# A decoder layer with product-key experts on one core: the gates stage's one-hots built for 8 tokens at a time in bf16

## The reference, cut to what matters

```
v1, i1 = lax.top_k(s1, PEER_TOPK);  v2, i2 = lax.top_k(s2, PEER_TOPK)
sc, ci = lax.top_k(cand, PEER_TOPK)          # cand: all sums v1 + v2
e1 = take(i1, ci // PEER_TOPK);  e2 = take(i2, ci % PEER_TOPK)
eid = e1 * N_KEYS + e2                       # N_KEYS = 128
gate = jax.nn.softmax(sc, axis=-1)
act = gelu(einsum('chkd,cd->chk', exp_u[eid], xc))
out = einsum('chk,chkd->cd', gate * act, exp_v[eid])
```

## Time and profile before

| | us |
|---|---|
| median of 3 executions | 2285.61 (2278.62 to 2299.04) |
| the profiled execution | 2285.57 |
| its span, first to last instruction | 2283.8 |
| TensorE / VectorE / ScalarE / GpSimd busy | 2038.0 / 1499.3 / 612.3 / 390.5 |
| the gates stage, first `hot` to `h_low` | 846.65 to 1034.73 |

### The profile page before, as it was taken

The page is one execution under the profiler, slowest core; times in us unless marked ns, Lnnn a source line. Parts: engine busy times, 40 slices in busy tenths (PEclk is TensorE's granted clock), DMA queues, the critical chain, the costliest instruction groups (busy, mean ns, idle before and its releaser), DMA issues. The chain is left out here.

```text
span 2283.8 us, 29284 instructions
## 1 busy us (share of the span) xinstructions
PE 2038.0 (89%) x9849; PEld 1774.4 (78%) x9849; DVE 1499.3 (66%) x3828; ACT 612.3 (27%) x1012; POOL 390.5 (17%) x473
## 2 busy tenths in 40 slices
PE   7997899999995029996699999999999999999994
PEld 6884566774773016665699999999999999999993
DVE  1122943102799989994777768767777777777773
ACT  2121323101111013332233333333333333333332
POOL 0000000000122220000322222222232222332320
PEclk9999556769997559998899999999999999999997
DMA  7002301220120003334877768878688786877853
GB/s 307 17 16 76 129 1 42 97 88 0 57 94 0 0 1 148 148 148 166 271 245 267 248 231 260 270 234 269 212 290 265 242 269 212 295 253 251 268 188 114
DMA packets 195603, 381.98 MB, mean 167 GB/s; under 512 B 12992, under 2 KB 134782, under 8 KB 192094
## 3 DMA queue, kind: packets, MB, share of 16 engines
q1 hardware_dynamic: 157557, 243.52, 30.8%
q0 software_dynamic: 36864, 134.23, 17.6%
q10 hardware_dynamic: 1056, 2.62, 0.3%
HBM read 345.21 MB, written 35.34 MB: 167 GB/s over the span
## 5 line engine op out<-in xcount | busy, mean ns | idle before, releaser
L1374 PE MATMUL a_ps<-h_high,u_high 128*128 128x416 f32 x1024 | 359.1, 351 | 42.2 <-DVE u_low L1513 40.0
L1392 PE MATMUL y_ps<-p_high,v_high 128*128 128x416 f32 x1024 | 359.7, 351 | 4.4 <-DVE v_low L1513 2.2
L1374 PE MATMUL a_ps<-h_low,u_high 128*128 128x416 f32 x1024 | 361.4, 353 | 0.0
L1392 PE MATMUL y_ps<-p_high,v_low 128*128 128x416 f32 x1024 | 360.5, 352 | 0.0
L1374 PE MATMUL a_ps<-h_high,u_low 128*128 128x416 f32 x1024 | 358.5, 350 | 0.0
L1392 PE MATMUL y_ps<-p_low,v_high 128*128 128x416 f32 x1024 | 358.2, 350 | 0.0
L1479 POOL DMA_INDIRECT rows<-in_u_rows,row_u x128 | 140.8, 1100 | 663.2 <-DVE dots L1566 326.3
L1479 POOL DMA_INDIRECT rows<-in_v,row_u x128 | 173.5, 1355 | 406.9 <-DVE y L1562 322.4
L1374 PEld LDWEIGHTS a_ps<-h_high,u_high 128*128 128x128 f32 x1024 | 192.9, 188 | 48.2 <-DVE u_low L1513 26.1
L392 PE MATMUL proj<-w_in_sb,xT 128*128 128x256 f32 (+1 forms) x880 | 193.5, 382 | 14.6 <-DVE xT L290 12.8
L1535 DVE TENSOR_TENSOR gel<-gel,gate 128x416 f32<-128x416 f32 x128 | 75.7, 591 | 197.2 <-ACT gel L1432 196.9
(11 more groups left out here) (194 smaller groups left out, 2769.7 us busy)
## 6 DMA issues: line engine op xcount, KB each, us to landing
u<-in_uT SPq DMA_DIRECT2D x128, 512.0 KB, 4.3
vv<-in_v SPq DMA_DIRECT2D x128, 512.0 KB, 4.7
gates_kept<-staged SPq DMA_DIRECT2D x13, 2048.0 KB, 6.2
gate<-gates_kept SPq DMA_DIRECT2D x32, 832.0 KB, 7.1
w_in_sb<-in_w_in SPq DMA_DIRECT2D x4, 2048.0 KB, 21.6
wq<-in_w_q SPq DMA_DIRECT2D x16, 512.0 KB, 3.3
ckT<-in_ckT SPq DMA_DIRECT2D x8, 768.0 KB, 5.7
cv<-in_cv SPq DMA_DIRECT2D x8, 768.0 KB, 5.3
```

Of the source, the lines that this page charges most:

```text
L1374: ins = pe.matmul(a_ps[c % 2][:, 0:DT], x[:, c % 2, k], y, start=(k == 0 and n == 0), stop=(k == KT - 1 and n == 2))
L1392: ins = pe.matmul(y_ps[m % 4][:, 0:DT], x[:, of % 2, c, at:at + P], y, start=(c == 0 and n == 0), stop=(c == CG - 1 and n == 2))
```

## The change

The 416 tokens are taken in 52 batches of TB = 8. Per batch DVE issues five tensor_tensor over 128x1024 in bf16 with the token as the innermost axis: `hot` (comparison of `count`, the numbers 0 to 127 each repeated 8 times, with `e1b`, the 8 tokens' values repeated for each number), `here` (the same with `e2b`), and three products of `here` with the three parts of the weight, `placed[..., 0 to 2]`. The weight is split ahead of the loop into three bf16 parts whose sum is the f32 value exactly (`w3`). PE then issues, per token, three bf16 products with the same `hot`, accumulated in the same quarter bank; a column of a token's tables lies 8 elements (16 bytes) behind the one before. The ring of `hot` is 4 batches, `placed` has 2. `staged` is moved over `gate`, `p_high` and part of `p_low`, which are not used in this stage, to make room.

```
-            for t in range(DT):
-                at = P + t
-                wait(dve, g_done, t - HOTS + 1)
-                nc.vector.tensor_scalar(hot[:, t % HOTS], iota_f[:], e1T[:, at:at + 1], None, ALU.is_equal)
-                nc.vector.tensor_scalar(placed[:, t % HOTS], iota_f[:], e2T[:, at:at + 1], wT[:, at:at + 1],
-                                        ALU.is_equal, ALU.mult).then_inc(hot_ready, 1)
+            nc.vector.tensor_copy(e1b[:], e1T[:])
+            nc.vector.tensor_copy(e2b[:], e2T[:])
+            nc.vector.tensor_copy(count[:], spread(iota_f[:].rearrange("p (k o) -> p k o", o=1), [P, NK, TB])
+                                  ).then_inc(w_split, 1)
+            nc.vector.tensor_copy(w3[:, 0], wT[:]).then_inc(w_split, 1)
+            dve.wait_ge(w_split, 2)
+            nc.vector.tensor_tensor(rest[:], wT[:], w3[:, 0], ALU.subtract).then_inc(w_split, 1)
+            dve.wait_ge(w_split, 3)
+            nc.vector.tensor_copy(w3[:, 1], rest[:]).then_inc(w_split, 1)
+            dve.wait_ge(w_split, 4)
+            nc.vector.tensor_tensor(w3[:, 2], rest[:], w3[:, 1], ALU.subtract).then_inc(w_split, 1)
+            dve.wait_ge(w_split, 5)
+
+            def batch(x, n):
+                return spread(x[:, P + n * TB:P + (n + 1) * TB].rearrange("p (o t) -> p o t", o=1), [P, NK, TB])
+
+            for n in range(BATCHES):
+                wait(dve, g_done, TB * (n - HOTS + 1))
+                nc.vector.tensor_tensor(hot[:, n % HOTS], count[:], batch(e1b, n), ALU.is_equal)
+                wait(dve, hot_ready, 2 * n)
+                nc.vector.tensor_tensor(here[:], count[:], batch(e2b, n), ALU.is_equal).then_inc(hot_ready, 1)
+                wait(dve, g_done, TB * (n - 1))
+                dve.wait_ge(hot_ready, 2 * n + 1)
+                for i in range(3):
+                    ins = nc.vector.tensor_tensor(placed[:, n % 2, i], here[:], batch(w3[:, i], n), ALU.mult)
+                ins.then_inc(hot_ready, 1)
...
-                pe.matmul(g_ps[bank % GBANKS][:, t % GT * NK:(t % GT + 1) * NK], hot[:, t % HOTS], placed[:, t % HOTS],
-                          start=True, stop=True).then_inc(g_done, 1)
+                for i in range(3):
+                    ins = pe.matmul(g_ps[bank % GBANKS][:, t % GT * NK:(t % GT + 1) * NK], hot[:, n % HOTS, :, at],
+                                    placed[:, n % 2, i, :, at], start=(i == 0), stop=(i == 2))
+                ins.then_inc(g_done, 1)
```

More of the change, by code:

```diff
@@ L61 @@
 GT = 4
+TB = 8
+BATCHES = DT // TB
 GB = 32
 NB = DT // GB
-HOTS = 6
+HOTS = 4
 GBANKS = 4
@@ L1244, in experts @@
         gates_kept = nc.dram_tensor("gates_kept", (NB, P, NK, GB), F32, kind="Internal").ap()
+        staged = nc.alloc_sbuf_tensor_at("staged", [P, 2, NK, GB], F32, offset=-(-nc.sbuf_base // 32) * 32)
         gate = sb("gate", [P, 2, NB, CG, GB])
-        staged = sb("staged", [P, 2, NK, GB])
         p_high = sb("p_high", [P, 2 * CG, DT], F32R)
@@ L1259, in experts @@
         coef_p = sb("coef_p", [P, FPP])
-        hot = sb("hot", [P, HOTS, NK])
-        placed = sb("placed", [P, HOTS, NK])
+        hot = sb("hot", [P, HOTS, NK, TB], BF16)
+        here = sb("here", [P, NK, TB], BF16)
+        placed = sb("placed", [P, 2, 3, NK, TB], BF16)
+        count = sb("count", [P, NK, TB], BF16)
+        e1b = sb("e1b", [P, T], BF16)
+        e2b = sb("e2b", [P, T], BF16)
+        w3 = sb("w3", [P, 3, T], BF16)
+        rest = sb("rest", [P, T])
         iota_f = sb("iota_f", [P, NK])
@@ L1273, in experts @@
         hot_ready, g_done, g_taken = sem("hot_ready"), sem("g_done"), sem("g_taken")
+        w_split = sem("w_split")
         gates_stored = [sem(f"gates_stored{b}") for b in range(2)]
@@ L1396, in _ @@
             for t in range(DT):
-                bank = t // GT
-                pe.wait_ge(hot_ready, t + 1)
+                bank, (n, at) = t // GT, divmod(t, TB)
+                pe.wait_ge(hot_ready, 2 * (n + 1))
                 if t % GT == 0:
                     wait(pe, g_taken, bank - GBANKS + 1)
-                pe.matmul(g_ps[bank % GBANKS][:, t % GT * NK:(t % GT + 1) * NK], hot[:, t % HOTS], placed[:, t % HOTS],
-                          start=True, stop=True).then_inc(g_done, 1)
+                for i in range(3):
+                    ins = pe.matmul(g_ps[bank % GBANKS][:, t % GT * NK:(t % GT + 1) * NK], hot[:, n % HOTS, :, at],
+                                    placed[:, n % 2, i, :, at], start=(i == 0), stop=(i == 2))
+                ins.then_inc(g_done, 1)
             pe.wait_ge(g_taken, DT // GT)
```

## The result

| | before | after |
|---|---|---|
| median us | 2288.49 (2278.62 to 2299.04, 4 runs) | 2401.45 (2379.46 to 2408.39, 4 runs) |
| the profiled execution's span | 2283.8 | 2377.4 |
| gates stage, from DVE's first instruction behind the two clears to the start of the last copy of `staged` | 846.65 to 1035.38 = 188.7 | 829.03 to 1128.74 = 299.7 |

The account below looks back on a forecast made before the run. DVE was taken to set the gates stage's pace: 2285.57 - 22.8 (DVE) + 2.3 (last burst) = 2265.1 us, plus one for small waits, forecast 2266. Range 2254 to 2292 (own case 2256 to 2272, chance 0.72).

Parts of the forecast that it names:

- DVE's new instructions: Gates stage, five per batch of 8 tokens: 0.68 us each, about 0.60 from start to start.
- The seven instructions ahead of the loop: DVE's copies, casts and subtractions before the gates loop, on the path: 3.6 us (bounds 3.6 and 4.2).
- The wait of `placed` for `here`: First `placed` of each batch waits for the instruction right ahead: 0.03 us, overlap lost, the pair costs 0.71.
- Rival 1: Gates loop on DVE: the wait for `here` costs 0.27 instead of 0.03, 12.5 us lost, 2278 us; chance 0.13.
- PE's price per pair: Weight load and matmul of 128 bf16 columns in the gates stage: 0.109 us, so a burst of 24 takes 2.6.
- The point from which PE binds: Gates loop: PE begins to bind at 0.130 us per pair; at 0.146 the whole gain is eaten.
- The second rival: Gates loop, PE becomes the bound: spread columns or 1.2 GHz, no overlap, pair up to 0.214, 2371 us; chance 0.10.
- The clock: PE's granted clock in the gates stage of the changed profile: expected at 1.00.
- The last burst: End of the gates stage, PE's uncovered final burst before the last copy: 2.9 us, or 2.3 us more than before.
- What follows the stage: Handover and expert stage after the last copy: unchanged, so what the last copy gains, the kernel's end gains.
- The gain that the change was built on: DVE's part of the gates stage ends 22.8 us sooner, at 0.389 us per token in the loop against 0.452.
- rivals 2 and 3: Rival 3: DVE runs its new instructions at one element per step, 5.8 us per batch, 2405 us; chance 0.05.

Follow-up runs that it names:

- the kernels with a fast reader: The changed kernel with PE's moving operand read from neighbouring columns: both operands neighbouring 2276.09 us, only the moving operand 2275.31 us.
- the kernel with GpSimd: The changed kernel laid out in runs of 4 tokens (columns 8 bytes apart), third product's table made on GpSimd instead of DVE: 2335.08 us, ratio 1.0184.
- the experiment with one product of three: The changed kernel with only the first of a token's three products read 16 bytes apart, the other two from neighbouring columns: 2278.91 us (1 run).

## Why the prediction was wrong, point by point

- **DVE's new instructions**: right. 0.685 us each (0.68 forecast), 0.60 from start to start, by the row of `hit` with the same type and form. The seven instructions ahead of the loop took 832.74-829.03 = 3.7 us (3.6 forecast).
- **The wait of `placed` for `here`**: too small. 0.79 from start to start, not 0.71. In the changed kernel's first batch, where `placed` waits for `here` alone, the gap behind `here` was 0.04 (833.35+0.68 to 834.07). With neighbouring columns, from the third batch on, where it waits for `g_done` too, the gap was 0.11 (932.41+0.68 to 933.20), though those products had long been done. My sum had one wait at 0.03; the batch came to 3.20 in place of 3.11: 52*0.09 = 4.7 us. That the second wait makes the difference is read from where the gap changes, and it holds only with `here` right ahead: with `hot` between, the same two waits left no gap. Rival 1, with 0.27, would have been more; the truth lay between. This is the reason why the kernels with a fast reader came out at 172 and not at 168.2, the 188.7-22.8+2.3 of my sum.
- **PE's price per pair**: this is the step that failed. I took 0.109 from the nearest row in shape, the turns of line 380, and bounded it by 0.058 and 0.218. The row's columns lie side by side, and its 128 f32 columns are read at 4 bytes; the new operand's lie 16 bytes apart. I had written that no row tests this, and then let a row that differs in just this point give the value. For neighbouring columns my value was twice too high (0.056 measured, my bound from below), for the spread ones less than half: 0.234, above even my upper bound. What failed is the step by which a burst is 2.6 us, lies under DVE's 3.11 and hides behind the next batch: it took 5.62 us and set the pace of all 52 batches. The point from which PE binds, 0.130 per pair, fits: at 0.118 the time is DVE's, at 0.234 it is PE's.
- **The second rival** was the right mechanism in its first part and came out near in size: 2371 forecast, 2401 measured, by a loop of 52*5.62 = 292 us where I had 267. That it came so near is in part luck: it doubled a pair of 0.107, which was itself twice too high, while the spread operand made four times the 0.056; and the missing overlap of load and matmul that it also asked for is ruled out. The spread operand alone makes the 0.234, at 0.50, and 0.23 to 0.24 at 1.00. Since I thought that several things had to come together, I gave it one chance in ten.
- **The clock**: I expected 1.00 in the stage. From 900 to 1000 us it was 0.50 wherever all products were spread, and 1.00 with neighbouring columns or columns 4 or 8 bytes apart in batches of 8, but for the kernel with GpSimd (0.59); with batches of 16 it was 0.90. The 0.50 of the changed kernel cost nothing by itself there, as the experiment with one product of three and the first bursts show.
- **The last burst**: 2.3 us more was forecast, for 0.109 per pair. With PE behind, it became 9.4 us from `h_low` to the last copy, four banks of backlog.
- **What follows the stage**: right, nothing changed (1248 and 1249 us).
- The gain that the change was built on is there, 17 us of stage as soon as the columns lie 4 bytes apart, 15 at 8 bytes.
- Two slips in the numbers change nothing: rivals 2 and 3 together have 0.15, not 0.14, and the "0.107 of a full-clock pair" in rival 2 is the 0.109 of line 380.

## What to carry to other kernels

Ask of every matmul how far apart, in bytes, the columns of its moving operand lie. A layout that makes a neighbour engine's instruction long and dense (token innermost) can make PE's operand sparse, and PE then pays: up to 16 bytes in proportion to the distance from 4 bytes on, to about four times the price of neighbours for bf16 in these runs; runs of two to four tokens gave DVE the same dense instructions and PE its full or half rate. And when a price is read off a nearest row, write down in which property the row differs: if it is the one that the change introduces, the row bounds nothing.

## What the runs showed of the hardware that I had not expected

- The price of 128 moving bf16 columns by their distance: 0.056 us (2 bytes), 0.058 (4), 0.118 (8), 0.234 (16), 0.23 to 0.24 (32). Spread weights cost next to nothing: 0.062 against 0.056 per pair.
- From 8 bytes on that price is the same at both levels of the clock: 0.234 at 0.50 and 0.23 to 0.24 at 1.00 for 16 bytes, 2.99 us at 0.50 and 3.02 at 1.00 for 24 products at 8 bytes. For neighbouring columns it is not: 0.106 at 0.50, 0.056 at 1.00. PE never idled in the records from 836 to 1128 us, and its clock sat at 1.2 GHz all the time.
- Of two bf16 tensor_tensor of DVE that ran beside one of GpSimd (2.40 us), the first took its usual 0.69 us, the second 2.38.
- Runs of only 2 bf16 elements with a broadcast source cost DVE nothing: its instructions had the same 0.69 us as with runs of 8.
